# Adding up a group's four pairs of experts on TensorE before the rows go to a table in DRAM

## What is computed

```
def hier_moe(h, w_grp, b_grp, w_rtr, b_rtr, w1, w3, w2):
    ...
    g_prob, g_sel = lax.top_k(grp_prob, 1)
    ...
    e_prob, e_sel = lax.top_k(jax.nn.softmax(in_grp, axis=-1), TOP_K_IN_GROUP)
    gate = g_prob * e_prob / jnp.sum(e_prob, -1, keepdims=True)
    ...
    hid = jax.nn.silu(jnp.einsum('td,edf->tef', t, w1)) * jnp.einsum('td,edf->tef', t, w3)
    y = jnp.einsum('tef,efd->td', hid * combine[..., None].astype(hid.dtype), w2)
...
        h = layer_norm(DEEPNORM_ALPHA * h + ffn, ln2_g[l], ln2_b[l])
```

## Time and profile before

| | us |
|---|---|
| median of 3 executions | 1487.41 |
| lowest and highest | 1486.31, 1493.91 |
| the profiled execution's own time | 1496.33 |
| its span, first to last instruction | 1494.5 |
| PE busy (PEld, DVE, ACT, POOL) in the span | 1362.4 (885.0, 578.2, 458.9, 69.6) |
| mean granted clock of TensorE | 0.958 of full |
| share of the chain that ended last: PE, DVE, ACT, issue | 76%, 15%, 5%, 4% |
| HBM read, written | 303.81 MB, 20.25 MB |

### The profile page before, as it was taken

The page is one execution under the profiler, slowest core; times in us unless marked ns, Lnnn a source line. Parts: engine busy times, 40 slices in busy tenths (PEclk is TensorE's granted clock), DMA queues, the critical chain, the costliest instruction groups (busy, mean ns, idle before and its releaser), DMA issues.

```text
span 1494.5 us, 17563 instructions
## 1 busy us (share of the span) xinstructions
PE 1362.4 (91%) x6735; PEld 885.0 (59%) x6735; DVE 578.2 (39%) x1211; ACT 458.9 (31%) x1001; POOL 69.6 (5%) x76
## 2 busy tenths in 40 slices
PE   6999989999999999989998979898998979998986
PEld 5777577774788877555333323687876644333332
DVE  2235213252477484331221115578575231221214
ACT  3245322362452234321111112463234312112211
POOL 0000000000012000000010000002100000100000
PEclk9999999999899999979999999799999979999999
DMA  9643162332330132554999998231032555999993
GB/s 366 166 155 113 57 228 85 113 113 110 121 112 31 57 114 85 197 199 175 420 421 423 421 410 348 75 113 57 29 112 86 225 197 229 420 421 423 419 422 153
DMA packets 52584, 314.55 MB, mean 210 GB/s; under 512 B 7886, under 2 KB 8398, under 8 KB 21136
## 3 DMA queue, kind: packets, MB, share of 16 engines
q1 hardware_dynamic: 44128, 287.56, 48.9%
q0 software_dynamic: 7184, 15.95, 3.4%
q10 hardware_dynamic: 1184, 9.84, 1.7%
HBM read 303.81 MB, written 20.25 MB: 217 GB/s over the span
## 4 chain that ended last, share of the span: by engine, by line
PE 76%; DVE 15%; ACT 5%; issue 4%; DMA 0%; DVEq 0%; ACTq 0%; SPq 0%
PE ps L990 22%; PE ps L1600 16%; PE ps L1627 8%; PE ps L1236 4%; PE ps L1024 4%; PE ps L1654 3%; PE ps L1438 1%; PE ps L1429 1%; PE ps L1495 1%; PE ps L1647 1%; PE ps L1686 1%; PE ps L1443 1%; DVE projT L2469 1%; PE ps L1198 1%; DVE small L2468 1%
## 5 line engine op out<-in xcount | busy, mean ns | idle before, releaser
L990 PE MATMUL ps<-hT,ring 128*128 128x272 f32 (+1 forms) x2016 | 490.2, 399 | 7.0 <-ACT projT L1806 3.2
L990 PEld LDWEIGHTS ps<-hT,ring 128*128 128x128 f32 x2016 | 387.7, 196 | 88.0 <-issue 11.3
L1600 PE MATMUL ps<-ring,arena 128*64 128x512 f32 x528 | 167.9, 629 | 12.9 <-issue 12.9
L2791 DVE TENSOR_TENSOR arena<-arena,ps 128x256 f32<-128x256 f32 x32 | 13.5, 422 | 296.6 <-ACT arena L2164 296.6
L1600 PE MATMUL ps<-projT,arena 128*64 128x512 f32 x368 | 123.9, 598 | 3.1 <-issue 2.0
L1627 PE MATMUL ps<-ring,arena 128*64 128x512 f32 x288 | 88.8, 602 | 9.0 <-issue 9.0
L1600 PEld LDWEIGHTS ps<-ring,arena 128*64 128x64 f32 x528 | 48.5, 144 | 79.9 <-issue 79.7
L1915 ACT ACTIVATE projT<-ps 128x272 f32<-128x272 f32 x68 | 27.0, 398 | 149.9 <-PE ps L990 148.4
L1627 PE MATMUL ps<-projT,arena 128*64 128x512 f32 x192 | 66.9, 604 | 6.6 <-issue 5.2
L1600 PEld LDWEIGHTS ps<-projT,arena 128*64 128x64 f32 x368 | 35.6, 136 | 50.0 <-issue 49.9
L2168 ACT ACTIVATE arena<-ps 128x256 f32<-128x256 f32 x32 | 12.3, 384 | 159.6 <-PE ps L1609 159.6
(11 more groups left out here) (467 smaller groups left out, 1803.4 us busy)
## 6 DMA issues: line engine op xcount, KB each, us to landing
ring<-experts SPq DMA_DIRECT2D x102, 1024.0 KB, 19.6
projT<-experts SPq DMA_DIRECT2D x70, 1024.0 KB, 20.6
ring<-w_in SPq DMA_DIRECT2D x64, 1024.0 KB, 5.0
ring<-w_out SPq DMA_DIRECT2D x16, 1024.0 KB, 5.0
prm<-experts SPq DMA_DIRECT2D x16, 1024.0 KB, 21.4
chosen<-arena POOLq DMA_DIRECT2D x2, 2176.0 KB, 21.7
prm<-params ACTq DMA_DIRECT2D x2, 2048.0 KB, 7.9
arena<-experts SPq DMA_DIRECT2D x4, 1024.0 KB, 8.0
```

The source lines that it names most:

```text
L990: mm = pe.matmul(ps[:, 5 + j % banks, 0:ncols], w[:, j % 2, k, :], hT[:, k, T - ncols:T], start=(k == 0), stop=(k == KC - 1))
L1600: mm = pe.matmul(ps[64 * e:64 * e + 64, 0, :], xg[:, 4 * h + k, i % 2, 64 * e:64 * e + 64], w[e][:, k // 2, 512 * (k % 2):512 * (k % 2) + ...
```

## The change

The table has one row for a token. All 16 pairs are now treated as the last four were: `rows_out` is a plain copy, `turn_pairs` and `add_up` run for every group, and the sums of a group, one row for each of its tokens, are copied to `xy` by DVE (left half) and ACT (right half) and sent by POOL for the first three groups. `slot_codes` and what read it are gone, with the wait for `rows_sent` before a buffer of `xo` is written. Banks 6 and 7 now hold sums, so the gather of two pairs uses banks 2 and 3 only and is cut in two (`gather_two`), one half before `down` and one behind it; the last two pairs are gathered together as well. `add_up(i - 2)`, `turn_pairs` and `turn_group` stand between the halves of `up`. In the first block nothing is changed. The filling of the table with zeros at the start and the reading back are halved in bytes. `chosen_added` has one add a tile and stands before the last `rows_out`.

```
-SENT = EXPERTS // 2 - PER_GROUP // 2
+SENT = GROUPS - 1
...
-        chosen = [nc.dram_tensor(f"chosen_{l}", (2 * T, D), F32, kind="Internal").ap() for l in range(LAYERS)]
+        chosen = [nc.dram_tensor(f"chosen_{l}", (T, D), F32, kind="Internal").ap() for l in range(LAYERS)]
...
-            return 2 <= i < PAIRS - 2
+            return i >= 2
...
-                        pe.wait_ge(s("pair_rows_copied"), 2 * (PAIRS_A_GROUP * g - 2))
+                        pe.wait_ge(s("pair_rows_copied"), 2 * (PAIRS_A_GROUP * g - 3))
...
+                def gather_two(i, half):
+
+
+                    q = i % PAIRS_A_GROUP
+                    if half == 0:
+                        rows_ready(i)
+                        if q == 2:
+                            pe.wait_ge(s("pairs_turned_copied"), i // PAIRS_A_GROUP + 1)
+                    pe.wait_ge(s("pair_tokens_copied"), copies_of(i - 1) + half)
+                    for k in range(4):
+                        mm = pe.matmul(ps[:, 2 + k // 2, (k % 2) * 2 * P:(k % 2 + 1) * 2 * P],
+                                       xrows[:, (4 * half + k) * P:(4 * half + k + 1) * P], psel[:, 2 * q:2 * q + 4, :],
+                                       start=True, stop=True)
+                    mm.then_inc(s("pair_gathered"), 1)
...
+                        tr = pe.transpose(ps[:, 2, P * q:P * (q + 1)], pselw[:, 2 * q:2 * q + 2, :], ident)
...
-                    q = i - SENT
+                    g, q = i // PAIRS_A_GROUP, i % PAIRS_A_GROUP
                     if q == 0:
-                        pe.wait_ge(s("slot_codes_read"), GROUPS - 1)
+                        pe.wait_ge(s("pairs_turned_copied"), g + 1)
+                        if g:
+                            pe.wait_ge(s("group_sums_copied"), 2 * g)
...
                         up_half(i, 0)
                         if i:
                             turn(i - 1)
-                        else:
-                            slot_codes(0)
-                        if q == 3 and g + 2 < GROUPS:
-                            slot_codes(g + 1)
-                        elif q == 3 and g + 2 == GROUPS:
-                            turn_pairs()
+                        if i > 1:
+                            add_up(i - 2)
+                        if q == 1:
+                            turn_pairs(g)
+                        if q == 2 and g + 1 < GROUPS:
+                            turn_group(g + 1)
                         up_half(i, 1)
+                        if i % 2 and i + 1 < PAIRS:
+                            gather_two(i + 1, 0)
                         if i:
                             down(i - 1)
-                        if i + 1 < PAIRS and (i % 2 or not together(i)):
-                            gather_pair(i + 1)
-                        if i > SENT:
-                            add_up(i - 1)
-                        if q == 2 and g + 1 < GROUPS:
-                            turn_group(g + 1)
...
                     turn(PAIRS - 1)
+                    add_up(PAIRS - 2)
                     down(PAIRS - 1)
                     add_up(PAIRS - 1)
...
+                    def sums_in(g):
+
+                        a.wait_ge(s("pair_summed"), 2 * g + 2)
+                        if SENT * l + g:
+                            a.wait_ge(sums_sent, 16 * (SENT * l + g))
+                        if g == GROUPS - 1:
+
+                            a.wait_ge(s("group_sums_copied"), 2 * g + 1)
+                        a.activation(xy[:, 512:D], ps[:, 7, :], ACT.Copy).then_inc(s("group_sums_copied"), 1)
...
-                            gate_sigmoid(i)
-                            if i + 1 < PAIRS and (i % 2 or not together(i)):
-                                tokens_in(i + 1)
                             if q == 2 and g + 2 == GROUPS:
                                 turned_in()
+                            if q == 1 and g:
+                                sums_in(g - 1)
+                            gate_sigmoid(i)
+                            if i == 0 or i % 2 and i + 1 < PAIRS:
+                                tokens_in(i + 1)
...
-                    if g:
-
-                        VP(v.tensor_reduce(mx[:, 0:1], xplaces[:, 2 * PER_GROUP:3 * PER_GROUP], AX, ALU.add))
-                        VP(v.tensor_scalar(group_tokens[:, g:g + 1], mx[:, 0:1], -0.5, float(NO_ROW - T // 2), ALU.mult, ALU.add),
-                           s("group_tokens_ready"))
-                    if g < GROUPS - 1:
-                        return
+                    VP(v.tensor_reduce(mx[:, 0:1], xplaces[:, 2 * PER_GROUP:3 * PER_GROUP], AX, ALU.add))
+                    VP(v.tensor_scalar(group_tokens[:, g:g + 1], mx[:, 0:1], -0.5, float(NO_ROW - T // 2), ALU.mult, ALU.add),
+                       s("group_tokens_ready"))
+
+                def weigh_pairs(g):
+
...
-                        elif 2 <= i < SENT + 2:
-                            v.wait_ge(rows_sent[i % 2], 16 * (SENT // 2 * l + i // 2))
                         x = xo[:, i % 2, 512 * half:512 * half + 512]
-                        if i < SENT:
-                            w = slot_weights[:, i // PAIRS_A_GROUP % 2, i % PAIRS_A_GROUP:i % PAIRS_A_GROUP + 1]
-                            v.tensor_scalar(x, ps[:, 4 + half, :], w, None, ALU.mult).then_inc(s("pair_rows_copied"), 1)
-                        else:
-                            v.tensor_copy(x, ps[:, 4 + half, :]).then_inc(s("pair_rows_copied"), 1)
-
-                def sums_in():
-
-                    v.wait_ge(s("pair_summed"), 1)
+                        v.tensor_copy(x, ps[:, 4 + half, :]).then_inc(s("pair_rows_copied"), 1)
+
+                def sums_in(g):
+
+                    v.wait_ge(s("pair_summed"), 2 * g + 1)
+                    if SENT * l + g:
+                        v.wait_ge(sums_sent, 16 * (SENT * l + g))
                     v.tensor_copy(xy[:, 0:512], ps[:, 6, :]).then_inc(s("group_sums_copied"), 1)
...
-                    for t in tiles:
+                    for t in norm_order(l):
                         n = ROWS[t]
                         VC(v.scalar_tensor_tensor(out=res[0:n, t, :], in0=res[0:n, t, :], scalar=ALPHA,
-                                                  in1=chosen_rows[t][0:n, 0, :], op0=ALU.mult, op1=ALU.add))
-                    for t in tiles:
-                        n = ROWS[t]
-                        VC(v.tensor_tensor(res[0:n, t, :], res[0:n, t, :], chosen_rows[t][0:n, 1, :], ALU.add))
...
-                    slot_codes_in(0)
+                    weigh_pairs(0)
                     select(1)
                     for i in range(PAIRS):
                         g, q = i // PAIRS_A_GROUP, i % PAIRS_A_GROUP
-                        if q == 3 and g + 2 < GROUPS:
-                            slot_codes_in(g + 1)
-                        elif q == 3 and g + 2 == GROUPS:
-                            pairs_in()
+                        if q == 1:
+                            if g:
+                                sums_in(g - 1)
+                            pairs_in(g)
+                        if q == 2 and g + 1 < GROUPS:
+                            select_pairs(g + 1)
                         hidden(i)
                         if i:
                             rows_out(i - 1)
-                        if i == SENT + 2:
-                            chosen_added(VP)
                         if q == 2 and g + 1 < GROUPS:
-                            select_pairs(g + 1)
+                            weigh_pairs(g + 1)
                             if g + 2 < GROUPS:
                                 select(g + 2)
+                    chosen_added(VP)
                     rows_out(PAIRS - 1)
-                    sums_in()
+                    sums_in(GROUPS - 1)
...
+            def send(l, group):
+
+                g.wait_ge(s("group_sums_copied"), 2 * group + 2)
+                if group:
+                    g.wait_ge(sums_sent, 16 * (SENT * l + group))
+                elif l == 0:
+                    g.wait_ge(zeros_out, 16 * LAYERS)
+                g.indirect_dma_start(chosen[l], bass.IndirectOffsetOnAxis(ap=group_tokens[:, group:group + 1], axis=0),
+                                     xy, None, bounds_check=T - 1, oob_is_err=False).then_inc(sums_sent, 16)
...
-                for i in range(SENT):
-                    if i % PAIRS_A_GROUP == 2:
-
-                        group = i // PAIRS_A_GROUP + 1
+                for group in range(GROUPS):
+                    g.wait_ge(s("group_tokens_ready"), group + 1)
+                    if group:
                         g.wait_ge(rows_stored, 16 * (3 * l + len(tiles_of(l))))
-                        g.wait_ge(s("group_tokens_ready"), group)
                         if group > 1:
                             g.wait_ge(rows_fetched, 16 * ((GROUPS - 1) * l + group - 1))
                         g.indirect_dma_start(xrows, None, normed_rows,
```

(16 more changed lines are left out.)

103 lines of the change are left out of this document (39 added, 64 removed).

## The result

| | before | after |
|---|---|---|
| median of 5 executions, us | 1490.78 | 1477.44 |
| lowest and highest | 1486.31, 1493.91 | 1475.00, 1479.99 |
| ratio of the times, 95% interval | | 0.9915 (0.9893 to 0.9936) |
| the profiled execution, its span | 1496.33, 1494.5 | 1477.59, 1475.8 |
| expert stage, layer 0 and layer 1 | 234.1, 233.4 | 230.1, 228.2 |

What follows compares the result with a forecast made beforehand. TensorE was taken to bound each expert stage's first half, weights the second. Layer 0 -3.3 and layer 1 -4.2, with 1.0 left over, gave -6.5 us; the median, between 1480.9 and 1489.8, was taken as 1484, range 1475 to 1491.

Steps and rivals of the forecast that it cites:

- (e): TensorE, each layer: `add_up` for 12 more pairs at 1.72 us each, 20.6 us added.
- (f): TensorE, each layer: `turn_pairs` for three more groups at 0.44 us, 1.3 us added.
- (b): TensorE, each layer: `turn_group`'s wait behind `down` for DVE's copy of bank 5 goes, three times 0.9, 2.7 us.
- (d): Stage end: `add_up(14)` moves between `turn` and the last `down`, covering ACT's copy; 0.7 us removed a layer.
- (c): Last two pairs: gathered together in 3.65 us instead of apart at 1.98 each; 0.3 us removed a layer.
- (a): TensorE, each layer: `slot_codes` removed, three times 0.79 us, 2.4 us.
- Do the waits go?: Expert stages: TensorE's waits for weights and the low clock go, with 0.5 us a layer left over.
- The 1.0 us that I left over: Both stages: estimated remainder of waits and low clock, 0.5 us a layer, counted against the gain.
- 17 us of backlog: Weights' queue: some 17 us to give up before a DMA engine idles, from 20.1 us landing against 2.5 us transfer.
- the first (the stage stays bound by DMA, 1477.5): Expert stages: only bytes count, 4.6 to 5.3 us gained a layer, median 1477.5; chance 0.17.
- The third, a wash: Low clock comes back elsewhere or the queue isn't lightened as claimed; 1487 within 3; chance 0.16.
- the second, that weights slip: Expert stages: slots free later, so waits return; 1509 if all return, 1498 if half; chance 0.12.

Runs made afterwards that it cites:

- more matmuls: Kernel before with four 256-column matmuls more in each of pairs 2 to 13, results unread; ratio 1.0016, stages 233.7 and 233.5 us.
- 2 MB back: Changed kernel with one 640 KB DRAM-to-DRAM copy on POOL's queue behind each of three sends a layer; ratio 0.9961, stages 233.3 and 230.5 us.
- places late: Changed kernel with `turn_group`, `select_pairs` and `turned_in` back behind the second gather; ratio 1.0034, stages 238.1 and 236.7 us.
- second bank: Changed kernel with pair 1's `up` writing PSUM bank 6 instead of bank 0; ratio 0.9898.
- 3.9 MB back: Changed kernel with three 640 KB DRAM-to-DRAM copies behind each of the first two sends a layer; ratio 1.0032, stages 241.0 and 237.0 us.
- few sums: Changed kernel with 9 of its 16 sums a layer left out; ratio 0.9886, stages 228.4 and 227.0 us.
- bytes taken out: Kernel before with its 12 sends writing nothing and the table read once for a token; ratio 0.9893, stages 225.9 and 224.5 us.

## Why the prediction was right or wrong

The forecast of 1484.0 was 6.6 us too high, and the range of 1475 to 1491 held the time. Part of that is luck: the five executions of before had a median 3.4 us above the 1487.41 that the forecast starts from, and with the ratio of 0.9915 that median would give 1474.8, just outside. The gain forecast was 3.4 us, where 12.7 and 8.5 were measured. I gave 0.59 to no more than half a per cent either way; the outcome was faster by more than that, which had 0.29. Point by point:

- **What bounds the stage before: wrong for its first half.** I read the chain as bound by TensorE up to 797.8 us and by weights behind it. The experiments show the DMA engines as the bound over the whole stage: 21 us of work on TensorE, from pair 2 on, were free (more matmuls), in a part that the chain calls gapless. The sum still came out, for it compared TensorE's new length with the old end of the stage, and that is right under either reading.
- **Added to TensorE, (e) and (f): right.** 16 sums of 1.72 us (2.03 the last), turnings of 0.44.
- **Removed from TensorE: undersized in sum, with errors both ways.** (b) was priced at 0.9 us a time. In the chain of before a DVE piece of 0.76 us stands there each time, and the wait around it brings it to 1.03; the places of layer 1 also fell from 0.60 to 0.36 us. (d), from the start of the last but one `down` to the end of `back`, was 14.02 us (913.33 to 927.35) and is 12.97 (903.66 to 916.63), so 1.0 in place of 0.7. (c) came out the other way: the gathers took 25.9 us before and 26.9 now, since a half of the cut gather takes 1.92 us and an uncut one 3.65, so 1.1 us more in place of 0.3 less. Of (a) only two of the three slot codes lie in the stage, 1.6 us in place of 2.4. In return the halves of `up` and the `down`s, without the low clock, are 2.2 us shorter in all: one behind a wait takes 3.65 us, where it takes 3.43 or 3.58 without. In all TensorE's own time grew by 15.2 and 14.9 us (230.1 less 234.1, plus the 14.6 and 4.6 that went, and the same in layer 1), where I had 15.9.
- **Do the waits go? Right, and better than forecast.** All of them went, and the lower clock. (One of the two slow groups of layer 0, 5.28 us at 835.70, was not behind a wait for weights: ahead of it stood the third stall behind `down`, 1.03 us, and the places. The moved places took it away as much as the waits that went; at what price each, no run shows.) The 1.0 us that I left over wasn't there. The stages gave 4.0 and 5.2, forecast -3.3 and -4.2 less the 1.0: 9.2 in place of 6.5.
- **DMA: right in kind.** POOL's queue at 2.89 MB (forecast 2.8). But I spoke of 17 us of backlog; putting 2 MB back showed in full but for 1.7 us in layer 0 and 2.6 in layer 1. The landing time of a weight shows a backlog, and yet the DMA floor lies only 1.7 and 1.2 us under the stage. A DMA share under 1.0 in the later stretches did not come: it reads 1.02 and 1.01. I had named it as the sign to tell the rivals apart, and it can't: from 700 to 900 us it is 1.00 to 1.02 in every kernel here, also in the one with the places late, whose stage is 8 us longer than the change's and which moved 406 GB/s in that stretch where the change moved 417.
- **New waits: right.** No wait of TensorE for DVE or ACT. The reads of the table began at 880.98, 5.4 us later than before, forecast 10. The zeros brought nothing: where the clock didn't dip, kernels of before begin pair 1's `up` at 684.8 to 687.1 us and changed ones at 686.0 to 686.7 (684.3 with the second bank).
- **The step that failed: from the profiled execution to the median.** "It is 8.9 us above the median, and the trace doesn't say where" was true of one trace. I took part of it for waits in the stages, and raised 1480.9 to 1484. The stages of layer 0 take 234.1 and 234.2 us in two profiles, while pair 1's start shifts by 8 us with the low clock ahead of it. None of it was in the stages, so the full gain carries over. 1480.9 would have been the answer by my own sum, and 1478.2 with the 9.2 us measured.

Of the rivals, the first (the stage stays bound by DMA, 1477.5) comes nearest to the time measured, and it had the source right: DMA bound the whole stage before, and the lighter queue made room for the gain. In the changed kernel, though, the chain has no waits left, and undoing the places cost 8 us, which a stage bound by bytes would have hidden. Its 4.6 to 5.3 us a layer agree with the 4.0 and 5.2 by two errors that cancel: the bytes were worth 5.7 and 6.4, and TensorE took 1.7 and 1.2 of that. The third, a wash, is out, and the second, that weights slip, is refuted by the kernel with more matmuls.

**What stays open.** The first ratio gives 12.7 us and the second, from later executions, 8.5 (0.9943). Their intervals overlap (0.9924 to 0.9936), and the stages account for 9.2. The 3 us beyond it can be the chance of the clock, but no run shows that. Against pure chance speaks that in the four changed kernels measured side by side (2 MB back, 3.9 MB back, few sums, second bank) the ratio puts the whole 2 to 6 us lower, against before, than the stages do, each from one profile: few sums 17.0 us by the ratio and 12.2 by the stages, for one. The change may make low clock outside the stages rarer. Nor do the runs say why a DMA byte on POOL's queue cost more than its share (8.2 and 8.9 us for what its share put at 6.3), or why 2 MB put back returned less than half of the gain in layer 1.

## What to carry to other kernels

When one resource has 100% of its time and the next one 90%, price a trade by both floors and take the larger: here 228.4 us of DMA and 230.1 us of TensorE made 230.1 of 234.1. Work moved onto the second resource is free up to the first one's floor, and from there every stall on it costs its full price. A chain without gaps does not prove that its engine is the bound; add work to it, or take some away, and see whether the end moves. When time is taken away, look where the engine waits next before calling it the old bound: here the stall of one path came back as a wait for rows on another. Compare profiled stage lengths rather than whole executions where another part of the program has a clock that dips by chance.

## What the runs showed of the hardware

- The DMA engines of one core, which carried weights from HBM to SBUF with a few per cent of other traffic, moved 424 and 408 GB/s in the two stretches shown, with TensorE busy for 20.00 us of 20 beside them. The Trainium skill (DMA: Bandwidth & Descriptors, section Where 436 GB/s comes from) puts the bound of such loads at about 358 GB/s a core; here, with one core at work, the measurement disagrees as it did before the change.
- Matmuls on the lower level (1.2 GHz, not 2.4) followed waits of 2.0 to 3.3 us in the stages. In both profiles of the kernel before and in the one with its bytes taken out they also followed the places of the last group, which stand behind a stall of 1.03 us. Behind waits it was 5.29 us in place of 3.58 behind a wait of 2.13, 5.35 behind one of 2.61, 6.54 in place of 3.65 behind 3.23. Not each such wait brought them: behind 2.31 us (2 MB back) and 2.82 us (few sums, before a `down` at 887.00) the next group took 3.65 at full clock. Without waits, as in the changed kernel, none was seen in a stage.
- In the first block the clock dipped with TensorE busy for 39.6 us of 40, in some executions and not in others, and the stages of the three profiles with most low clock ahead began 5 to 9 us later than the others.
- The landing time of the same 1 MB in layer 0's stage was 18.4 to 20.6 us where the DMA engines bound it, 9.5 to 13.2 where TensorE had no wait for weights, 14.3 where it had two short ones. In layer 1 up to 15.4 went with no wait. The DMA share from 700 to 900 us was 1.00 to 1.02 in all kernels.
